# Output projection of a decoder step: sample heads and mixing as one stage of nine written tiles, output weights loaded into the last page places, routing products on four column groups

## What is computed

```python
h = rms_norm(x, g_mix)
qd, kd, vd, qs, ks, vs = split(h @ w_in)
o = concat(diff_attention(qd, kd, vd), stick_breaking_attention(qs, ks, vs))   # 1024 wide
x1 = x + o @ w_out
h2 = rms_norm(x1, g_ffn)                # x1 * rsqrt(mean(x1^2) + eps) * g_ffn
gl = h2 @ w_group + b_group             # 4 groups
el = h2 @ w_erouter + b_erouter         # 4 x 4 experts
y = x1 + experts(h2, top-1 group, top-2 experts of it)
y = rms_norm(y, g_final)
# outputs: y, and the new keys and values
# inside diff_attention, last step, for each head:
o = o * rsqrt(mean(o * o) + 1e-5) * subln_g * (1 - lambda_init)
```

## Time and profile before

| | us |
|---|---|
| median of three runs | 1770.45 |
| lowest and highest run | 1767.7, 1771.8 |
| profiled execution, its time | 1765.44 |
| its span | 1763.4 |
| stage of the sample heads | 1083.96 to 1102.24 |
| mixing stage | 1102.24 to 1279.88 |
| first product of the mixing | 1109.00 |

### The profile page before, as it was taken

How to read it: one execution, slowest core, us unless ns; L and a number is a source line. 1 busy time by engine, 2 the same in 40 slices (tenths; PEclk the granted TensorE clock), 3 DMA queues, 4 the chain that set the end, 5 groups by cost and what they waited for, 6 DMA issues and landing times. The chain is left out here.

```text
span 1763.4 us, 28766 instructions
## 1 busy us (share of the span) xinstructions
PE 1371.7 (78%) x8924; PEld 1028.3 (58%) x8924; DVE 815.7 (46%) x1133; ACT 719.8 (41%) x1106; POOL 268.1 (15%) x200
## 2 busy tenths in 40 slices
PE   6999999958878777489788884788825988899930
PEld 4777787745555554356555552676724766777720
DVE  7021112105454545266657576222254655667635
ACT  5121211205454455255445454112104666677721
POOL 1000000000000000000000000000003545556644
PEclk6999999979999899799999996788856999999975
DMA  5333213137778786277787763423106898652248
GB/s 184 92 114 125 90 42 125 65 126 234 251 218 259 219 252 207 94 242 249 220 254 221 249 205 120 157 95 115 75 24 247 306 347 347 236 186 96 108 166 311
DMA packets 166803, 320.73 MB, mean 182 GB/s; under 512 B 20455, under 2 KB 59914, under 8 KB 162570
## 3 DMA queue, kind: packets, MB, share of 16 engines
q1 hardware_dynamic: 153818, 276.09, 47.2%
q0 software_dynamic: 7200, 26.22, 4.1%
q10 hardware_dynamic: 5648, 16.78, 2.4%
HBM read 313.33 MB, written 56.56 MB: 210 GB/s over the span
## 5 line engine op out<-in xcount | busy, mean ns | idle before, releaser
L1964 PE MATMUL gate_up_ps<-w_gate_up_split,slot_rows_T 128*128 128x512 f32 x768 | 194.8, 412 | 30.8 <-DVE slot_rows_T L2016 30.6
L2008 DVE TENSOR_TENSOR w_gate_up_split<-w_gate_up,w_gate_up_split 128x2048 fp32r<-128x2048 f32 x64 | 143.8, 2289 | 130.3 <-ACT w_gate_up_split L2062 130.3
L1932 POOL TENSOR_TENSOR w_down_split<-w_down,w_down_split 128x2048 fp32r<-128x2048 f32 x32 | 170.5, 5328 | 161.1 <-ACT w_down_split L2070 161.1
L927 PE MATMUL turns_and_scores_ps<-ident,pages 128*128 128x128 f32 (+1 forms) x1088 | 150.7, 283 | 55.4 <-DMA pages<-in_cache_d 26.3
L1964 PEld LDWEIGHTS gate_up_ps<-w_gate_up_split,slot_rows_T 128*128 128x128 f32 x768 | 149.6, 198 | 69.0 <-DVE slot_rows_T L2016 37.3
L255 PE MATMUL proj_ps<-w_in_hi,h_T_hi 128*128 128x512 f32 x432 | 174.2, 403 | 9.4 <-DVE w_in_lo L305 9.4
L927 PEld LDWEIGHTS turns_and_scores_ps<-ident,pages 128*128 128x128 f32 (+1 forms) x1088 | 123.5, 148 | 98.7 <-issue 98.3
L255 PE MATMUL proj_ps<-w_in_lo,h_T_hi 128*128 128x512 f32 x432 | 171.0, 396 | 0.0
L255 PE MATMUL proj_ps<-w_in_hi,h_T_lo 128*128 128x512 f32 x432 | 170.8, 395 | 0.0
L2062 ACT ACTIVATE w_gate_up_split<-w_gate_up 128x2048 fp32r x64 | 119.1, 1908 | 117.2 <-DMA w_gate_up<-in_w_up 88.6
L350 ACT ACTIVATE proj_rows<-proj_ps,sum_squares 128x512 f32<-128x512 f32 x54 | 37.0, 688 | 277.8 <-PE proj_ps L255 260.7
(11 more groups left out here) (220 smaller groups left out, 2154.7 us busy)
## 6 DMA issues: line engine op xcount, KB each, us to landing
pages<-in_cache_d SPq DMA_DIRECT2D x256, 256.0 KB, 3.1
pages<-in_cache_s SPq DMA_DIRECT2D x256, 256.0 KB, 3.1
w_gate_up<-in_w_gate SPq DMA_DIRECT2D x32, 1024.0 KB
w_gate_up<-in_w_up SPq DMA_DIRECT2D x32, 1024.0 KB
w_down<-in_w_down SPq DMA_DIRECT2D x32, 1024.0 KB
scratch_moe_out<-expert_out ACTq DMA_DIRECT2D x32, 512.0 KB
w_in_now<-in_w_in SPq DMA_DIRECT2D x48, 256.0 KB, 4.4
x_tiles<-in_x SPq DMA_DIRECT2D x9, 512.0 KB, 4.6
```

What stands on the lines that cost most here:

```text
L927: last = pe.transpose(kT_ps[:, KIND_BLOCKS * e + b, 0:n], rows[0:n, e, b, :], t.ident[0:n, 0:n])
L1932: pool.tensor_tensor(dn_split[:, u, 1, :, :], w_dn[:, bass.ds(at, 1), :, :].rearrange("p a k n -> p (a k) n"), dn_split[:, u, 0, :, :].bit ...
L1964: last = pe.matmul(gu_ps[:, u, :], xT[:, u, a, k, :], gu_split[:, u, b, k, :], start=(k == 0 and m == 0), stop=(k == KC - 1 and m == 2))
L2008: dve.tensor_tensor(gu_split[:, u, 1, at, :].rearrange("p k (c n) -> p k c n", c=2), raw[:, at, :, :], gu_split[:, u, 0, at, :].bitcast(F3 ...
```

## The change

The two stages become one, `mix_out`, with its nine tiles written out instead of looped.

- The page places are allocated once for both attentions. After the last page load of the stick-breaking attention SyncE's `load_next` goes on with the eight pieces of w_out, in places 0 to 7. x, x1 and h of the mixing live in places 8 to 13. The splitting of w_out is the first thing in the new stage, each piece of it released to TensorE by itself.
- The sample heads are computed inside the tile loop (VectorE's steps at tiles 1, 2, 4 and 5, TensorE's product at tile 3, ScalarE's Sqrt at tile 4) and are used as tile 8 from SBUF, without the way through DRAM.
- The high and low parts of oT are made one tile further ahead; the product has three PSUM places instead of four; the first half of tile n + 1's product is followed by the transposes of tile n, the second half by its routing products.
- What is transposed is x1, not h2. g_ffn is multiplied into the router weights beforehand, and rsqrt is applied when the logits are kept. The routing products have the router weights (32 columns, 20 of them in use) as the stationary side and 128 moving columns; four of the eight go to four column groups of the array at a time, and one more product with a fixed 128 x 32 matrix (`sum_map`) adds the four groups.

```diff
+            t.page_rows = att.enter_context(nc.sbuf_tensor("pages", [P, PAGE_PLACES, PAIR, KIND_BLOCKS, P], F32))
+            t.w_out_raw = t.page_rows[:, 0:BLOCKS, :, :, :].rearrange("p k e b n -> p k (e b n)")
...
                     if n < len(page_uses):
                         load_page(*page_uses[n])
+                    elif kind == STICK and n - len(page_uses) < BLOCKS:
+                        load_w_out(n - len(page_uses), n % PAGE_PLACES)
...
+            def _(sp):
...
+                load_o(0)
+                load_x(0)
+                load_o(1)
+                sp.dma_start(sum_map[:, :], t.sum_map).then_inc(r_loaded, 16)
...
+                    sp.dma_start(g_T[:, :], t.g_ffn.rearrange("(k p) -> p k", p=P)).then_inc(r_loaded, 16)
...
+                for n in range(TILES):
+                    load_o(n + O_PLACES)
+                    sp.wait_ge(x1_done, 2 * n + 2)
+                    sp.dma_start(t.x1[n * P:(n + 1) * P, :], x1[:, n % 2, :]).then_inc(x1_stored[n % 2], 16)
+                    load_x(n + 2)
+                    sp.wait_ge(h_done, n + 1)
+                    sp.dma_start(t.h2[n * P:(n + 1) * P, :], h[:, n % 2, :]).then_inc(h_stored[n % 2], 16)
...
+                def product(n, c):
+                    m = 2 * n + c
+                    if c == 0:
+                        pe.wait_ge(o_lo, n + 1)
+                    if m >= Y_BANKS:
+                        pe.wait_ge(x1_done, m - Y_BANKS + 1)
+                    for k in range(BLOCKS):
+                        if m == 0:
+                            pe.wait_ge(w_lo, k + 1)
...
+                def route_parts(n):
...
+                    for k0 in range(0, KC, GROUPS_OF_K):
+                        for j in range(GROUPS_OF_K):
+                            last = pe.matmul(parts_ps[ROUTE_COLS * j:ROUTE_COLS * (j + 1), 0:P],
+                                             w_route[:, k0 + j, :], xT[:, k0 + j, :],
+                                             start=(k0 == 0), stop=(k0 + GROUPS_OF_K == KC))
+                    last.then_inc(parts_done, 1)
...
+                for n in range(TILES):
+                    product(n, 0)
+                    if n >= 2:
+                        route_sum(n - 2)
+                    if n >= 1:
+                        turn(n - 1)
+                    product(n, 1)
+                    if n >= 1:
+                        route_parts(n - 1)
+                    if n == 3:
+                        pe.wait_ge(step, SUMMED)
+                        pe.matmul(ms_ps[:, 0:N], t.ones[:, :], s_sq[:, :], start=True, stop=True).then_inc(sums, 1)
+                turn(LAST)
+                route_sum(LAST - 1)
+                route_parts(LAST)
+                route_sum(LAST)
...
+                low_o(0)
+                for k in range(BLOCKS):
+                    dve.wait_ge(w_hi, k + 1)
+                    dve.tensor_tensor(w_split[:, 1, k, :], t.w_out_raw[:, k, :], w_split[:, 0, k, :].bitcast(F32),
+                                      ALU.subtract).then_inc(w_lo, 1)
+                low_o(1)
+                dve.memset(w_route[:, :, :], 0.0).then_inc(route_ready, 1)
+                dve.wait_ge(r_loaded, 16 * 6)
...
+                for n in range(TILES):
+                    residual(n, 0)
+                    if n >= 2:
+                        keep_logits(n - 2)
+                    residual(n, 1)
+                    low_o(n + 2)
+                    h_rows(n)
...
+                high_o(1)
+                for n in range(TILES):
+                    if n >= 1:
+                        keep_turned(n - 1)
+                        keep_parts(n - 1)
+                    high_o(n + 2)
+                    square_sum(n)
```

More of the change, by code:

```diff
@@ L1381 @@
 ALL = TILES * P
[L1384 to L1399 removed]
 def row_tile(dram, tile):
     return dram[bass.ds(tile * P, P), :]
+Y_BANKS = 3
+O_PLACES = 2
+ROUTE_COLS = COL_TILE
 def mix_out(nc, t):
@@ L1430, in mix_out @@
+        x, x1, h = (rows[:, BLOCKS + 2 * n:BLOCKS + 2 * n + 2, :] for n in range(3))
+        xT = sb("x1T_tile", [P, KC, P])
+        parts = sb("logit_parts", [P, P])
         square = sb("square2", [P, D_MODEL])
         ss = sb("sum_squares2", [P, 2, 3])
-        y_ps = ps("mix_out_ps", [P, 2, 2, BANK])
-        hT_ps = ps("h2T_ps", [P, 2, BANK])
+        s_oT = sb("sample_oT", [P, BLOCKS, P])
+        s_mix = sb("sample_diff", [P, DEC_BATCH, H_DIFF, DEC_SEQ])
+        s_sq = sb("sample_diff_sq", [P, N])
@@ L1500, in route @@
-                def route(it, u):
-                    pe.wait_ge(h_done.sem, h_done.after(it, u))
+                def product(n, c):
[7 more added lines that the diff above has]
+                            pe.wait_ge(w_lo, k + 1)
+                        for i, (a, b) in enumerate(((0, 0), (1, 0), (0, 1))):
+                            last = pe.matmul(y_ps[:, m % Y_BANKS, :], oT_split[:, n % 2, a, k, :],
+                                             w_split[:, b, k, c * BANK:(c + 1) * BANK],
+                                             start=(k == 0 and i == 0), stop=(k == BLOCKS - 1 and i == 2))
+                    last.then_inc(y_done, 1)
@@ L1507, in route @@
-                        last.then_inc(hT_done.sem, 1)
-                    pe.wait_ge(hT_kept.sem, hT_kept.after(it, 2 * u + 1))
-                    pe.wait_ge(lg_kept.sem, lg_kept.after(it, u - 1))
-                    for k in range(KC):
-                        last = pe.matmul(lg_ps[:, 0:N_LOGITS], hT[:, k, :], w_route[:, k, :],
-                                         start=(k == 0), stop=(k == KC - 1))
-                    last.then_inc(lg_done.sem, 1)
-                out(0, 0)
-                pe.wait_ge(r_loaded, 16 * 5)
@@ new lines, in _ @@
+                low_o(0)
[6 more added lines that the diff above has]
+                dve.wait_ge(r_loaded, 16 * 6)
+                dve.wait_ge(route_ready, 1)
+                for k in range(KC):
+                    dve.tensor_scalar_mul(w_route[:, k, 0:N_LOGITS], w_rows[:, k, :], g_T[:, k:k + 1]).then_inc(route_ready, 1)
@@ L2291, in host_constants @@
             "before_const": before, "token_const": token,
+            "sum_map": np.tile(np.eye(COL_TILE, dtype=np.float32), (P // COL_TILE, 1)),
             "column_const": np.arange(P, dtype=np.float32)}
```

421 lines of the change are left out of this document (203 added, 218 removed).

## The result

| | before | after |
|---|---|---|
| median of the runs, us | 1771.12 (4 runs) | 1711.78 (4 runs) |
| lowest and highest | 1767.7, 1785.44 | 1703.53, 1714.77 |
| ratio of the runs, 95% interval | | 0.965 [0.959, 0.970] |
| span of the profiled execution | 1763.4 | 1701.7 |

The change makes the kernel 59 us faster. The page of the changed kernel, part 1, answers to the earlier trace rows: the counts hardly move, and TensorE is busy for 26 us less.

What follows compares the result with a forecast made beforehand. TensorE's program order and waits were taken to bound the stage; first tile done 1108.1, second 1121.1, seven more at 13.2 to 1213.5, end 1223.9 against 1279.88: 56 us less, 1714 us, range 1706 to 1730.

Steps and rivals of the forecast that it cites:

- The tile: Output projection loop: 13.2 us a tile against 18.8 before, bounds 12.7 and 14.2, with no wait on TensorE.
- allowance of 0.3 for changes of kind: TensorE in each tile: four changes between kinds of matmul cost 0.3 us in all, bounds 0 and 0.8.
- rival (d): Tile loop: TensorE waits each tile for a high half ScalarE holds back, at most 20 us, 1734; chance 0.04.
- rival (a): Tile loop: the clock still falls once a tile, costing 15 to 22 us, 1729 to 1736; chance 0.13.
- the two waits bring the loss of clock: Kernel before, tile loop: waits of 0.90 and 1.65 us bring the granted clock from 1.00 to 0.50.
- The drain of which the Trainium skill speaks: TensorE tiling mode changes, two a tile: at five times 0.11 us, a tile 0.8 longer and the sum 6 us.
- The start: Start of the merged stage: first product can start at 1092.0 against 1109.00 before, first tile done at 1108.1.
- before it stood on the path: Sample heads' work, 2.3, 1.0 and 3.2 us on VectorE and 1.3 on ScalarE, now lies in the tiles' slack.
- taking the w_out loads out of the stretch: Stage start: w_out loads follow the attention's last page loads, hiding their eight issues of 4.15 us too.
- The cold start: First tile's second half costs 1.3 us over 5.6 after TensorE is about half busy, bounds 0 and 2.8.
- Rival (b): DMA loop sets the tile, or late w_out or router holds the start: 5 to 15 us, 1719 to 1729; chance 0.09.
- The tail: End of the stage: next stage starts 10.4 us after the last product, against 13.9 after the last addition before.

Runs made afterwards that it cites:

- e4: Changed kernel with the logits as eight products straight into one PSUM place, without column groups: tile 13.61 us against 12.82, stage 6.8 us longer, median 1712.58 us.
- e3: Changed kernel with transposes, routing parts and sum in one run behind both product halves: tile 14.04 us, stage 9.9 us longer, median 1722.34 us.
- e5: Kernel before, with only the attention tile's high and low parts made a tile earlier: stage 19.1 us shorter, median 1758.64 us, ratio 0.990 to before.
- e1: Changed kernel with the sample heads' work at the front of the stage: first product 1.0 us later, stage 0.6 us longer, median 1713.87 us.
- e2: Changed kernel with the w_out loads issued in the new stage, behind the first attention tile's load: stage 1.0 us longer, median 1716.62 us.
- e8: Changed kernel with the first product waiting until all eight w_out pieces are split: first product after 22.1 us, stage 6.2 us longer, median 1712.87 us.
- e9: Changed kernel with samples, w_out loading and splitting, then attention tile in series at the start: first product after 28.6 us, stage 12.8 us longer, median 1721.81 us.
- e7: Changed kernel with four w_out pieces split before the first attention tile: stage 1.7 us shorter, median 1707.64 us, ratio 0.962 to before.
- e6: Changed kernel with four w_out pieces split first and 22 identity products on TensorE during the initial load: stage 4.2 us shorter, median 1711.95 us.

## Why the prediction was right, point by point

The forecast was 56 us less and 1714; measured were 59 less and 1712, by the stage's own length 60.3. None of the rivals came true. The 4.3 us that the forecast missed are 3.4 in the tiles and 1.4 in the start, less 0.5 in the tail.

**The tile: 13.2 forecast, 12.82 measured.** The view that carried it, the halves of a product read off VectorE's two additions, was right to 1%: 5.62 and 5.66 for 5.60. Parts 0.58 for 0.55 (the choice by the nearest row, half of it for half the columns, was good), sum 0.14 for 0.25, transposes 0.82 for 0.9. The allowance of 0.3 for changes of kind is in the products' and transposes' rows already and comes to about 0.2 by e4. No wait, as forecast: ScalarE's high half, for which rival (d) had TensorE wait, is a tile ahead.

**The clock** stayed at 1.00 (2.4 GHz) over all eight tiles behind the first; rival (a) was priced at 15 to 22 us and is void. It leaned on the Trainium skill, TensorE: Matmul & The Clock Gate, the section on psum-queue depth-cycling. That section tells of a kernel in which TensorE idles briefly between its groups of products; here the products go through three PSUM places in turn with no idle time between them and without a swing, so its case did not arise. The argument in the prediction, that without waits there is nothing to bring the clock down, fits the changed kernel. That the waits had to go altogether is not so: in e3 two waits of 0.74 and 0.40 us a tile did not bring it down either. So the prediction's sentence on the kernel before, that the two waits bring the loss of clock, is shown in part only. By e5 the wait of 1.65 is part of the cause: without it two of seven falls go, and half of what the low clock costs (14.9 to 7.7 us). What brings about the other half is open.

**Changes of tiling mode.** The parts start without a gap. The 24 products ahead of them take 5.66 us (1129.43 - 1123.77) where those ahead of e4's logits take 5.54, and the products behind them 5.62 against 5.57. The drain of which the Trainium skill speaks (TensorEngine Tiling (Array Packing), Key Properties) costs no more than these 0.2 us here.

**The start: the sum was nearly right, two of its reasons were not.** First tile's product done 30.0 us after the last kept sample rows by the forecast (1108.1 - 1078.09), 28.6 measured. Two sentences of the step fell. One is that of the sample heads' work, "before it stood on the path": in the kernel before, VectorE was through with it at 1091.3, but the last piece of w_out landed only at 1098.28; high and low half of that piece (1.06 and 1.2) end the splitting at 1100.6. And e1 puts the work back at the front for 0.6 us, because 5 us of load time cover most of it.

```profile
1098.28 1.06 ACT L1366 ACTIVATE w_out_split<-w_out_raw 128x1024 fp32r<-128x1024 f32 x1 [0.45 <-DMA w_out_raw<-in_w_out]
```

The other is that the change gains by taking the w_out loads out of the stretch: e2 puts them back for 1.0 us. What gained is the overlap: products go by pieces behind the splitting (e8: 6.2), and the attention tile's load, w_out and the samples are no longer one behind the other (e9: 12.8 in all, of 16.0). The loads' and the sample heads' cover can each go, since another hides the same time; with all of them the gain goes. The prediction came near the right end times because it walked the new order, step by step, instead of adding up what each edit saves; the two wrong reasons did not enter its sum.

**The cold start** is the term of the start that was mis-sized: 1.3 us were given to the second half tile, and it cost nothing. The first half tile ended where the forecast had it, 23.1 us after the copy of the last sample rows (1101.2 - 1078.09; measured near 1099.2, less 1076.14), and the second took 5.5 us at a clock of 1.00 instead of 6.9. The clock was at 0.50 up to about 1095.2, but the first half waited for the last pieces of w_out anyway: the last was split at 1098.40, and its products start at 1098.45. Where the pieces come sooner the half clock does show: e7 and e6 differ by it, 2.5 us.

**The loads.** The 4-byte load of g_T, for which the prediction had no row, landed 3.2 us after its issue, well inside its cover. The loads of the attention tiles (median 4.9) made ScalarE wait once, for the first tile. Rival (b) is void.

**The tail:** 10.4 us after the last product forecast, 10.9 measured (1217.60 - 1206.72). Two misses offset each other in part: the last scaled rows end 4.95 after the last product (1209.68 + 1.99) instead of 5.7, and what follows them takes 5.9 instead of 4.7.

## What to carry to other kernels

Where TensorE needs a result that another engine must first copy, put part of a long product in between: here half a product of 5.6 us hid the copies that cost 1.2 us a tile when e3 put the routing back in one run. A wait before matmuls costs more than it shows where the clock falls after it: by e5 here 1.65 us of wait a tile cost itself and, on average, another 1.0 in slower products. At the start of a stage look for what can go in pieces, and walk the new order to its end time; what single edits save there does not add up, since one can hide behind another. And when neighbouring stages vary from run to run by more than the effect, compare the stage's length in the profile, not the run.

## What the runs showed of the hardware

The same attention program took up to 21 us longer in one profiled execution than in another. The copy of the last sample rows came at 1070.73 in e4 and at 1091.89 in e1, and in the windows over the second attention the mean granted clock is nearly the same, but TensorE is busy for longer:

```profile
738.00:1091.00 353.00, 279.99 (x2815) 186.90 (x2816) 216.24 (x231) 166.96 (x261) 0.00 (x0) 0.90 0.72 228
```

```profile
724.00:1070.00 346.00, 276.23 (x2817) 184.04 (x2817) 216.44 (x232) 166.96 (x261) 0.31 (x1) 0.91 0.73 233
```

The first is e1, the second e4. VectorE's and ScalarE's work is the same to 0.2 us. TensorE's is 3.8 longer, the stretch 7 longer; what lies ahead of it, the input projection and the first attention, makes up the other 14. What starts it was not tested.
